# Down projection of the experts in three fp32r passes, and two raw weight buffers reused for the last stage's rows

## What is computed

```
def _grouped_experts(xt, eid, wts, w_gate, w_up, w_down):
    ...
    def expert_block(args):
        xblk, ex = args
        h = jax.nn.silu(xblk @ w_gate[ex]) * (xblk @ w_up[ex])
        return h @ w_down[ex]
    yb = lax.map(expert_block, (xb, blk_e)).reshape(P, D)
    ...
    return jnp.einsum("tkd,tk->td", y_slot.reshape(T, TOP_K, D), wts)
...
    y_moe = _hier_moe(u, w_rg, w_re, w_e_gate, w_e_up, w_e_down)
    x = _layer_norm(DEEPNORM_ALPHA * x + gate2 * y_moe, ln_g[1], ln_b[1])
```

## Time and profile before

| | us |
|---|---|
| median of 3 runs (1967.32 to 1971.78) | 1971.23 |
| the profiled execution | 1972.89 |
| its span | 1971.3 |
| expert stage, first transposes to last `y_sb` | 1313.3 to 1847.0 |
| last stage, barrier to end | 1855.8 to 1971.3 |
| PE busy, share of the span | 89% |

### The profile page before, as it was taken

One profiled execution on the slowest core, in us unless ns is written; L12 is line 12 of the kernel. 1 busy time (PEld: TensorE's weight loads), 2 busy tenths in 40 slices (PEclk: granted clock), 3 DMA queues, 4 the chain that ended last, 5 costly groups with the idle time before them and its releaser, 6 DMA issues. The chain is left out here.

```text
span 1971.3 us, 29175 instructions
## 1 busy us (share of the span) xinstructions
PE 1759.8 (89%) x9140; PEld 1372.8 (70%) x9141; DVE 1109.0 (56%) x1724; ACT 614.5 (31%) x754; POOL 586.8 (30%) x685
## 2 busy tenths in 40 slices
PE   5999999999999999999689996029999999999674
PEld 3888878888888899999478884026665677666321
DVE  3566655556666766565567664504455333455198
ACT  2333322232333222222211110104465433455142
POOL 0122222111222222102154443443343333344155
PEclk7999999999999999999799997569999999999897
DMA  8544344444333232331764443428899865798495
GB/s 248 150 129 127 104 119 140 129 120 122 97 94 94 86 86 62 89 105 39 231 192 151 149 139 119 165 77 277 297 343 343 305 233 170 232 326 301 189 393 180
DMA packets 302075, 342.74 MB, mean 174 GB/s; under 512 B 19078, under 2 KB 257447, under 8 KB 299538
## 3 DMA queue, kind: packets, MB, share of 16 engines
q1 hardware_dynamic: 278872, 284.30, 44.8%
q0 software_dynamic: 18000, 55.87, 7.9%
q10 hardware_dynamic: 5106, 1.31, 0.4%
HBM read 276.86 MB, written 64.58 MB: 173 GB/s over the span
## 5 line engine op out<-in xcount | busy, mean ns | idle before, releaser
L1481 DVE TENSOR_TENSOR w_gu_lo<-w_gu_raw,w_gu_hi (+1 forms) x64 | 146.4, 2291 | 158.1 <-ACT w_gu_hi L1474 158.0
L895 DVE TENSOR_TENSOR w_lo<-w_raw,w_hi 128x1024 fp32r<-128x1024 f32 x112 | 137.9, 1234 | 139.4 <-ACT w_hi L545 136.6
L657 POOL TENSOR_TENSOR o_r<-o_ms,neg_half 128x4 f32<-128x4 f32 (+1 forms) x16 | 16.8, 1050 | 662.9 <-DVEq L931 662.9
L1967 PE MATMUL ph<-w_gu_hi,x_hi 128*128 (+1 forms) x408 | 179.3, 440 | 12.2 <-DVE hh L1929 9.7
L712 PE MATMUL pr<-ub_hi,w_hi 128*128 128x288 f32 (+1 forms) x672 | 189.2, 335 | 0.0
L712 PE MATMUL pr<-ub_hi,w_lo 128*128 128x288 f32 (+1 forms) x672 | 184.2, 328 | 0.0
L712 PE MATMUL pr<-ub_lo,w_hi 128*128 128x288 f32 (+1 forms) x672 | 183.6, 327 | 0.0
L712 PE MATMUL pr<-ua_hi,w_hi 128*128 128x512 f32 x448 | 183.0, 408 | 0.0
L1995 PE MATMUL py<-w_dn_w,hhT 128*128 x400 | 180.8, 594 | 1.9 <-ACT hhT L1899 1.0
L712 PE MATMUL pr<-ua_hi,w_lo 128*128 128x512 f32 x448 | 177.7, 397 | 0.0
L712 PE MATMUL pr<-ua_lo,w_hi 128*128 128x512 f32 x448 | 177.5, 396 | 0.0
(11 more groups left out here) (332 smaller groups left out, 3446.6 us busy)
## 6 DMA issues: line engine op xcount, KB each, us to landing
w_raw<-in_w_in SPq DMA_DIRECT2D x112, 512.0 KB, 4.2
w_gu_raw<-in_w_e_gate SPq DMA_DIRECT2D x32, 1024.0 KB, 8.4
w_gu_raw<-in_w_e_up SPq DMA_DIRECT2D x32, 1024.0 KB, 11.3
w_dn_w<-in_w_e_down SPq DMA_DIRECT2D x32, 1024.0 KB, 9.8
w_mod<-in_w_mod SPq DMA_DIRECT2D x16, 1024.0 KB
y_t<-y_scratch SPq DMA_DIRECT2D x16, 1024.0 KB, 7.2
w_ring<-in_w_mod SPq DMA_DIRECT2D x4, 2048.0 KB, 17.4
x_cols<-in_x_prompt SPq DMA_DIRECT2D x32, 256.0 KB, 5.3
```

What stands on the lines that cost most here:

```text
L657: pool.tensor_tensor(o_r[:, 0:c], o_ms[:, 0:c], keep["neg_half"][:, 0:c], ALU.pow).then_inc(o_rs, 1)
L895: dve.tensor_tensor(w_lo[:, n % WS], w_raw[:, n % WRAW], w_hi[:, n % WS].bitcast(F32), ALU.subtract).then_inc(lo_done, 1)
L1481: dve.tensor_tensor(w_slot(keep["gu_lo"], s, lo, hi), w_slot(keep["gu_raw"], r, lo, hi), w_slot(keep["gu_hi"], s, lo, hi).bitcast(F32), AL ...
L1967: last = pe.matmul(ph[:, :], x[:, half, k * P:(k + 1) * P], w_slot(w, s, k * GU, (k + 1) * GU), start=(k == 0 and m == 0), stop=(k == KT - ...
```

## The change

The down projection is done in three passes like the others. ACT copies an expert's raw down weights to fp32r (`w_dn_hi`) and DVE makes the rest (`w_dn_lo`), 2048 elements a partition, once an expert and in two buffers. This is `split_down(e + 1)`, done in the last block of expert e, on both engines behind half 1 of the gate and up split and, on ACT, ahead of `y_sb`. The transposed hidden rows get a hi (ACT, as before) and a lo (DVE's new `hidden_low`), and the down projection now waits for DVE's part. SP's load of down weights waits for the split of the expert two before it, and there are two raw buffers in place of three; the third expert's down weights are loaded at the start of the expert stage and not while routing. The tile `gsil` is gone (the product goes into `gsig`).

The rows that the last stage needs (gate, norm scale and shift) and the first eight `x_t` tiles are loaded into the three `gu_raw` buffers when the last three experts' splits are done, and the last stage has separate semaphores for `y_t` and `x_t`.

```diff
@@ SP in the expert stage
                 def down(e, s):
-                    if not (isinstance(e, int) and e < RAW):
-                        wait_apart(sp, dn, blocks_before(sp, e - (RAW - 1)) + 1, tick)
+                    wait_apart(sp, dn_l, e - (RD - 1), tick)
                     wait_apart(sp, wd_in, 16 * e, tick)
                     load_down(sp, io, keep, e, s)
+                def tail(e, i, n, rows):
+                    sp.wait_ge(gu_l, 2 * e + 2)
+                    sp.dma_start(gu_raw[0:n, e % RAW, i * D:(i + 1) * D], rows).then_inc(tail_in, 16)
...
+                for t in range(EARLY):
+                    tail(NE - 2 + t // 4, t % 4, P, scr["x1"][t * P:(t + 1) * P, :])
@@ ACT
+                def split_down(e):
+                    act.wait_ge(wd_in, 16 * e + 16)
+                    act.activation(w_slot(dn_hi, slot(act, e, 2), 0, KD * D), w_slot(dn_w, slot(act, e, RD), 0, KD * D), ACT.Copy).then_inc(dn_h, 1)
...
                     if gu_next is not None:
                         split_gu(gu_next, 1)
+                    if dn_next is not None:
+                        split_down(dn_next)
                     act.wait_ge(dn, g + 2)
@@ DVE
+                def hidden_low(g):
+                    dve.wait_ge(hT_hi, g + 1)
+                    dve.tensor_tensor(hhT[:, 1], pht[:, 0:KD * P].rearrange("p (k t) -> p k t", k=KD), hhT[:, 0].bitcast(F32), ALU.subtract).then_inc(hT_sb, 1)
...
-                def block_work(g, gu_next):
+                def block_work(g, gu_next, dn_next=None):
+                    hidden_low(g)
                     x_evac(g + 2, dve.snap(g % 2))
                     gate(g + 1)
                     if gu_next is not None:
                         split_gu(gu_next, 1)
+                    if dn_next is not None:
+                        split_down(dn_next)
@@ PE
-                    pe.wait_ge(wd_in, 16 * e_now + 16)
+                    pe.wait_ge(dn_l, e_now + 1)
...
-                            last = pe.matmul(py[:, hf * 512:(hf + 1) * 512], hhT[:, k, :], w_slot(dn_w, s_down, at, at + 512),
-                                             start=(k == 0), stop=(k == KD - 1))
+                                last = pe.matmul(py[:, hf * 512:(hf + 1) * 512], hhT[:, i, k, :], w_slot(w, s, at, at + 512),
+                                                 start=(k == 0 and m == 0), stop=(k == KD - 1 and m == 2))
@@ last stage, SP and PE
-                        sp.wait_ge(xa_rdy, t - R + 1)
-                    sp.dma_start(x1[0:n, s, :], scr["x1"][t * P:t * P + n, :]).then_inc(in_[s], 16)
+                    if t >= EARLY:
+                        s = (t - EARLY) % R
+                        if t >= EARLY + R:
+                            sp.wait_ge(xa_rdy, t - R + 1)
+                        sp.dma_start(x1[0:n, s, :], scr["x1"][t * P:t * P + n, :]).then_inc(x_in[s], 16)
...
-                    pe.wait_ge(in_[s], 32 * (t // R) + 32)
+                    pe.wait_ge(y_in[s], 16 * (t // R) + 16)
```

More of the change, by code:

```diff
@@ L50 @@
 RAW = 3
+RD = 2
+EARLY = 8
 MC = 256
@@ L1539, in _ @@
                     if e:
-                        for landed in ("wg_in", "wu_in", "wd_in"):
+                        for landed in ("wg_in", "wu_in"):
                             sp.wait_ge(keep[landed], 16 * e)
+                        sp.wait_ge(keep["wd_in"], 16 * min(e, RD))
                     load_gate_up(sp, io, keep, e, e)
[L1543 to L1547, removed]
+                    if e < RD:
+                        load_down(sp, io, keep, e, e)
                 sp.wait_ge(tab_rdy, 1)
@@ L1787, in expert_loop, with expert @@
         def expert_loop(eng, split_gu, block_work):
-            def expert(e, gu_next):
+            def expert(e, gu_next, dn_next):
                 first = blocks_before(eng, e)
@@ L1797, in expert @@
                     split_gu(gu_next, 0, last)
-                block_work(last, gu_next)
+                block_work(last, gu_next, dn_next)
             with eng.Fori(0, NE - 2) as e:
-                expert(e, e + 2)
-            expert(NE - 2, None)
-            expert(NE - 1, None)
+                expert(e, e + 2, e + 1)
+            expert(NE - 2, None, NE - 1)
+            expert(NE - 1, None, None)
         with nc.Block() as block:
@@ L1814, in down @@
                 def down(e, s):
-                    if not (isinstance(e, int) and e < RAW):
-                        wait_apart(sp, dn, blocks_before(sp, e - (RAW - 1)) + 1, tick)
+                    wait_apart(sp, dn_l, e - (RD - 1), tick)
                     wait_apart(sp, wd_in, 16 * e, tick)
                     load_down(sp, io, keep, e, s)
+                def tail(e, i, n, rows):
+                    sp.wait_ge(gu_l, 2 * e + 2)
+                    sp.dma_start(gu_raw[0:n, e % RAW, i * D:(i + 1) * D], rows).then_inc(tail_in, 16)
                 sp.wait_ge(xg_in, 32)
-                gate_up(3, 0)
-                with sp.Fori(4, NE) as e:
+                gate_up(RAW, 0)
+                down(RD, 0)
+                with sp.Fori(RAW + 1, NE) as e:
                     gate_up(e, sp.snap(e % RAW))
-                    down(e - 1, sp.snap((e - 1) % RAW))
-                down(NE - 1, (NE - 1) % RAW)
+                    down(e - 1, sp.snap((e - 1) % RD))
+                down(NE - 1, (NE - 1) % RD)
+                for i, row in enumerate((scr["mod"][0, 3 * D:4 * D], None, io["ln_g"][0, 1], io["ln_b"][0, 1])):
+                    if row is not None:
+                        tail(NE - 3, i, P, row_bcast(row, P))
+                for b in range(DEC_B):
+                    sp.dma_start(gu_raw[b * DEC_L:(b + 1) * DEC_L, (NE - 3) % RAW, D:2 * D],
+                                 row_bcast(scr["mod"][b + 1, 3 * D:4 * D], DEC_L)).then_inc(tail_in, 16)
+                for t in range(EARLY):
+                    tail(NE - 2 + t // 4, t % 4, P, scr["x1"][t * P:(t + 1) * P, :])
+                sp.wait_ge(tail_in, 16 * (3 + DEC_B + EARLY))
             @block.gpsimd
@@ L2027, in combine_phase @@
         ps_n = ps("ps_n4", [P, D])
-        in_ = [sem("t4_in%d" % s) for s in range(R)]
+        y_in = [sem("y4_in%d" % s) for s in range(R)]
+        x_in = [sem("x4_in%d" % s) for s in range(R)]
         o_out = [sem("o_out%d" % s) for s in range(4)]
```

61 lines of the change are left out of this document (38 added, 23 removed).

## The result

| | before | after |
|---|---|---|
| median (range) | 1971.23 us (1967.32 to 1971.97) | 1980.64 us (1975.41 to 1985.34) |
| the profiled execution | 1972.89 | 1975.41 |
| ratio of medians, 95% interval | | 1.0046 [1.0033, 1.0059] |

The changed kernel is slower by 0.46%. The forecast of 1962 has the wrong sign, and 1980.64 lies outside its range of 1950 to 1975.

What follows compares the result with a forecast made beforehand. It took PE's 10.03 us a block and, in two stretches, nearly full DMA engines as bounds; 5.9 - 13.1 + 1.3 - 2.1 - 1 = -9.0 us, giving 1963.9 for the profiled execution, 1962 as median, range 1950 to 1975.

Steps and rivals of the forecast that it cites:

- Part 1: Down projection on PE: three passes take 2.73 us for 3.43, 0.70 less a block; blocks without stalls take 9.33.
- Part 2 (b): Down projection waits for hidden_low behind half 0 of DVE's split, which follows y_sb: one-block experts take 10.1 us a block.
- Part 2 (a): In an expert's last block y_sb waits for ACT's down copy, starting 4.3 us after the down projection's start, formerly 3.63.
- First stretch: Blocks 0 to 10: later y_sb and one-block experts cost more than other blocks save, +2.9 us in sum.
- Blocks 10 to 20: Weight loads start 5.1 us later and bind, hidden_low's path adds 0.8: block 20 is 5.9 us late, +3.0 here.
- rival B: Loads don't matter: later issue is caught up, first twenty blocks end where they did; 6 us less, 1956; chance 0.2.
- Blocks 20 to 39: 19 blocks at 9.33 us plus 0.6 of stall at each of three two-block experts: -13.1 us.
- the slack of 0.4 us: Experts of several blocks, last block: hidden_low would be done 0.4 us before PE is ready for the down projection.
- rival C: Scatter held by DVE's down split, then landing in 9 us; two-block experts take 22.6 us for 20.06; 1982; chance 0.1.
- Y + 6.0: Experts of several blocks: earliest down projection, 6.0 us after the previous y_sb starts (Y), through half 0 and hidden_low.
- Blocks 39 to 47: One-block experts at 11.4, six of 10.1 and one of 9.33 us, plus 4.9 for late loads: +1.3 us.
- The end: Last three blocks have no gate and up split, -2.1 us; last stage's first matmul gets its load sooner, -1.

Runs made afterwards that it cites:

- e1_ids: Changed kernel with two slots for ids_cur, copied before POOL waits for the scatter's landing: 1968.24 us, ratio 0.9994.
- b1_ids: Kernel before with two slots for ids_cur, copied ahead of the wait for the scatter's landing: 1963.86 us, ratio 0.9967.
- e4_nolow: Changed kernel without hidden_low, the third pass reading the high part of the hidden rows: 1964.07 us, ratio 0.9966.
- e5_nodn: Changed kernel with DVE's down split cut from 2048 to 64 elements, second pass reading the high part: 1967.35 us, ratio 0.9989.
- e6_none: Changed kernel with ids_cur in two slots, no hidden_low, and DVE's down split cut to 64 elements: 1950.0 us, ratio 0.9905.
- r_after: The changed kernel measured again, unaltered, in a second series: 1982.47 us, ratio 1.0064.

## Why the prediction was wrong, step by step

**Part 1** was right: 2.72 us for 2.73, and blocks of 9.3.

**Part 2 (b), one-block experts: the step that failed.** The prediction ran the path from `y_sb` over half 0 and `hidden_low` to the down projection and back, 10.1 us, and let the next `y_sb` wait for PE alone. Yet the earlier trace rows named another releaser: 3.67 us of waiting for `ids_cur`. The path from `y_sb` over DVE's half 1 and POOL's held copy back to `y_sb` is longer, 11.34, and it was in force before at 11.01. The prediction read those 11 us as landing and loads (which bound only the last blocks of the stretch). It also weighed the shared port for the scatter and passed by the copy of the ids, though a held copy of 1.65 us (of `ids_now`) stood in the earlier trace rows. So a one-block expert does not "gain nothing": it loses 0.33 where the loop ruled before, and 1.3 where it did not, as e1_ids, b1_ids and e4_nolow show from three sides. Within its own path the estimate was 0.5 short: 7.41 for 7.1 and 3.17 for 2.93. In the first part a handover was in no term: where PE waits for `hidden_low` in after, the matmul starts 0.38 to 0.42 us behind its end.

**Part 2 (a)** held: `y_sb` at 1582.78 is 4.1 us after the start at 1578.70; 4.3 was put. It held nobody up there.

**First stretch:** +5.3 (106.9 against 101.6) for +2.9. Blocks 1, 2, 7 and 10 begin 11.5 to 12.1 us after the block ahead of them; 11.4 and 11.5 were put.

**Blocks 10 to 20:** +2.8 for +3.0, right in size by the wrong cause. The loads did go out as late as predicted (7.6 and 8.9 us for 7.7 and 9.1), but no split idled over 1.0 us ahead of its data, the time of ACT's own loop instructions; e1_ids took 5.5 us from the stretch without touching a load. This is rival B's "the loads don't matter" in part, with a worse term in their place; that the size agrees is luck.

**Blocks 20 to 39: the costliest miss**, -3.7 for -13.1. Two terms failed. The first is the slack of 0.4 us in an expert's last block. The handover uses it up: from a `y_sb` to the down projection behind its half 0 it takes 6.3 us where 6.0 was put, which leaves nothing of 9.33. So each late `y_sb` counts, in experts of three blocks too: `y_sb` waited for scatters that took 7.0 and 6.8 us to land, and blocks 25 and 28 took 10.5 and 9.9. The last blocks of experts 16, 18 and 19 took 9.9 or 10.0 with the pause behind their down projection. Experts 16 to 19 together took 3.3 us over 9.33 a block. The second is the stalls of two-block experts, put at 1.8: the five blocks from 34 on took 54.5 us, 7.9 over 9.33 each. There rival C's mechanism is at work in part. POOL, ACT and PE in that stretch of after:

```profile
1703.46 1.01 POOL L1881 DMA_INDIRECT y_scratch<-y_sb,ids_cur  x1 [2.03 <-ACT y_sb L1926]
...
1712.09 0.19 POOL L1878 COPY ids_cur<-ids_ring 128x4 int32 x1 [4.42 <-DMA y_scratch<-y_sb,ids_cur]
1712.37 1.12 ACT L1926 ACTIVATE y_sb<-py,ids_cur 128x1024 f32<-128x1024 f32 x1 [6.17 <-POOL ids_cur L1878]
...
1718.66 0.72 PE L2030 MATMUL py<-w_dn_hi,hhT 128*128 x2 [3.58 <-DVE hhT L1948]
```

The scatter goes out beside the loads, unheld, and lands 8.6 us after the start of its issue, `y_sb` waits 6.17, and the block takes 13.0 us. C wanted this, with 9 us of landing, of all seven two-block experts; the trace has it in full once. Yet the landing is not new. ACT at the same block before:

```profile
1712.66 1.12 ACT L1906 ACTIVATE y_sb<-py,ids_cur 128x1024 f32<-128x1024 f32 x1 [6.53 <-POOL ids_cur L1864]
```

There the scatter took 8.85 us and `y_sb` waited 6.53, but the block took 10.7. What is new is what stands behind that `y_sb`: the down projection, by half 0 and `hidden_low`, 6.29 us later (the prediction's Y + 6.0). The prediction had that path, and reckoned with a landing of 7 where the rows of before had 8.7. The 11.05 us of the next block are in part the fallen clock: its down projection takes 4.44 us. e5_nodn and e4_nolow take 6.3 and 4.6 us from the stretch, e6_none 8.9 of the 11.2 over 9.33.

**Blocks 39 to 47:** +3.7 (in r_after +5.5) for +1.3, again 11.3 us a block and not 10.1.

**The end** was right: -1.5 for -1.4 from 47 to 49, -1.8 for -1.7 behind. The first matmul of the last stage on PE, after:

```profile
1864.20 11.07 PE L2172 MATMUL ps_y<-y_t,ident 128*128 128x512 f32 x19 [14.88 <-DMA y_t<-y_scratch]
```

The first of its loads is issued at 1859.34, so it waits 4.86 us; in the earlier trace rows 6.1 lay between issue and data. That is 1.3 for the 1 put.

**The sum.** In the profiled execution the stretches give +5.3 + 2.8 - 3.7 + 3.7 - 1.5 - 1.8 = +4.8, less 2.3 for the earlier start, +2.5. Predicted was -9.0. Of the 13.8 us between the two sums, 9.4 lie in 20 to 39 and 2.4 each in 0 to 10 and 39 to 47. The median lies 5 us above that execution. r_after's trace, 3.9 us longer, shows 2.5 of its own in blocks 10 to 20 and 39 to 47, where the granted clock fell three times more.

**What stays open.** Why a gate and up projection starts 0.4 us late behind an odd block's down projection that was only just in time: e5_nodn has it but once, and nothing here shows how PE's queue comes to it. And why the granted clock falls in some of these blocks and not in others that wait as long.

## What to carry to other kernels

Follow each wait of the path to its releaser and close the loop: the slowest cycle of dependences through all engines sets the period (11.34 us by `ids_cur`, 10.58 by `hidden_low`, 10.6 by the gate, as one after the other was taken away), and one in-order list that carries two unrelated jobs (here a copy of ids behind a landing, a small subtraction behind a large one) can close a cycle that nobody wrote. A saving on the busiest engine is worth what the second-slowest cycle allows, and every instruction that pays for it must be put on that cycle, at its place, before it is called hidden. When a wait is named in the rows that one quotes, price it, and look first whether it can be taken away for nothing: here two slots for a tile of four words gave more than the whole change.

## What the runs showed of the hardware

POOL's small copy is held by a DVE subtraction with both inputs in SBUF, to its end: 0.20 us alone, 2.01 us in the row at 1485.95. The prediction's rule from the Trainium skill (SBUF — State Buffer, section Who interferes with whom) says so, and the trace agrees. The issue of an indirect DMA on POOL is held as well: the scatter takes 1.01 us alone, 2.01 us at 1584.71 under DVE's down split, and is not held in e5_nodn, where that split is short; the gathers of rows in after take at most 1.00 us alone and up to 2.90 beside such a subtraction. Such an issue ends about 0.87 us behind the subtraction. The prediction had left this open.

TensorE's granted clock fell to its lower level seven times in the expert stages of after and r_after, each time near a down projection that PE had waited 1.8 to 4.1 us for. That down projection then held PE for 4.2 to 4.4 us, where the others of the two traces took 2.7 to 3.5.
